# Gate products with the recurrent branch's four channel groups and both layers' modulation products placed between them

## What is computed

```
u = conv_b + sum(xp[:, j:j + s] * conv_w[j] for j in range(C_CONV))
r = sigmoid(einsum(u, wa) + ba);  i = sigmoid(einsum(u, wx) + bx)
log_a = -LRU_C * r * softplus(-lam)
a = exp(log_a)
gated_in = sqrt(-expm1(2.0 * log_a)) * (i * u)
hs = associative_scan(combine, (a, gated_in))
y_c = hs * gelu(yc)
gates = sigmoid(gt + b_gate)                       # gt: 3072 of the columns of h @ w_in
mod = silu(cond) @ w_ada + b_ada                   # once for the even, once for the odd layer
shift, scale, gate = split(mod, 3)
```

## Time and profile before

| what | value |
|---|---|
| median of 3 runs | 4327.39 us (4327.06 to 4327.49) |
| the profiled execution's own time | 4331.49 us |
| its span in the trace | 4329.7 us |
| mean granted TensorE clock | 0.915 of full speed |
| PE busy, share of the span | 3607.7 us, 83% |
| DVE busy | 2302.6 us, 53% |
| ACT busy | 1458.5 us, 34% |
| POOL busy | 296.1 us, 7% |
| DMA | 229.97 MB, mean 53 GB/s |

### The profile page before, as it was taken

One profiled execution on the slowest core, in us unless ns is written; L12 is line 12 of the kernel. 1 busy time (PEld: TensorE's weight loads), 2 busy tenths in 40 slices (PEclk: granted clock), 3 DMA queues, 4 the chain that ended last, 5 costly groups with the idle time before them and its releaser, 6 DMA issues. The chain is left out here.

```text
span 4329.7 us, 44928 instructions
## 1 busy us (share of the span) xinstructions
PE 3607.7 (83%) x18492; PEld 2935.6 (68%) x18492; DVE 2302.6 (53%) x3898; ACT 1458.5 (34%) x2559; POOL 296.1 (7%) x379
## 2 busy tenths in 40 slices
PE   3799996877797999999789877877697888868877
PEld 2588885655675888888567666766575777756666
DVE  4899444666644222223555646656544666435554
ACT  3221133544212111111443534444323444423431
POOL 2121200000101000000100000000001000000000
PEclk9899968988898999999899989999797999988999
DMA  2133331000520111111201000000220010100111
GB/s 83 31 120 121 113 125 56 26 20 10 195 102 27 52 49 40 46 44 46 83 27 32 22 31 26 25 31 21 96 73 33 29 34 29 35 18 18 31 60 62
DMA packets 69292, 229.97 MB, mean 53 GB/s; under 512 B 8472, under 2 KB 12568, under 8 KB 69088
## 3 DMA queue, kind: packets, MB, share of 16 engines
q1 hardware_dynamic: 43056, 132.68, 9.3%
q0 software_dynamic: 22576, 81.85, 5.5%
q10 hardware_dynamic: 3456, 12.58, 0.8%
HBM read 180.42 MB, written 36.17 MB: 50 GB/s over the span
## 5 line engine op out<-in xcount | busy, mean ns | idle before, releaser
L2139 PE MATMUL PS<-m,m 128*128 128x512 f32 (+2 forms) x3560 | 1418.8, 399 | 286.9 <-DVE m L2483 54.9
L2140 PE MATMUL PS<-m,m 128*128 128x512 f32 (+2 forms) x3560 | 1378.1, 388 | 0.0
L2141 PE MATMUL PS<-m,m 128*128 128x512 f32 (+2 forms) x3560 | 1377.5, 387 | 0.0
L2139 PEld LDWEIGHTS PS<-m,m 128*128 128x128 f32 (+1 forms) x3560 | 687.5, 193 | 482.4 <-issue 111.5
L2141 PEld LDWEIGHTS PS<-m,m 128*128 128x128 f32 (+1 forms) x3560 | 687.5, 193 | 135.6
L2140 PEld LDWEIGHTS PS<-m,m 128*128 128x128 f32 (+1 forms) x3560 | 690.1, 194 | 119.6 <-issue 2.7
L2483 DVE TENSOR_TENSOR m<-m,m 128x1024 fp32r<-128x1024 f32 (+4 forms) x203 | 207.8, 1024 | 417.0 <-ACT m L2316 416.2
L2768 DVE TENSOR_TENSOR m<-PS,m 128x512 fp32r<-128x512 f32 x352 | 241.1, 689 | 287.4 <-ACT m L2410 286.9
L2410 ACT CAST m<-PS 128x512 fp32r<-128x512 f32 x352 | 205.6, 588 | 513.7 <-PE PS L2238 512.1
L2229 PE MATMUL PS<-m,m 64*128 64x256 f32 (+5 forms) x1968 | 257.8, 373 | 85.0 <-ACT m L2399 57.9
L2229 PEld LDWEIGHTS PS<-m,m 64*128 64x128 f32 (+1 forms) x1968 | 218.0, 201 | 130.8 <-ACT m L2399 73.7
(11 more groups left out here) (203 smaller groups left out, 3980.8 us busy)
## 6 DMA issues: line engine op xcount, KB each, us to landing
m<-in_w SPq DMA_DIRECT2D x220, 512.0 KB, 3.3
g_scratch<-m ACTq DMA_DIRECT2D x24, 512.0 KB, 2.8
m<-g_scratch POOLq DMA_DIRECT2D x24, 512.0 KB, 4.7
m<-in_w SPq DMA_DIRECT2D x32, 256.0 KB, 2.7
x_scratch<-m POOLq DMA_DIRECT2D x2, 4096.0 KB, 12.3
m<-m POOLq DMA_DIRECT2D x60, 128.0 KB, 2.7
y_scratch<-m POOLq DMA_DIRECT2D x12, 512.0 KB, 2.9
m<-y_scratch POOLq DMA_DIRECT2D x12, 512.0 KB, 5.3
```

The lines of the kernel that those rows point to most:

```text
L2139: pe.e.engine.matmul(o, L[0], X[0], start=start, stop=False)
L2140: pe.e.engine.matmul(o, L[0], X[1], start=False, stop=False)
L2141: return pe.e.engine.matmul(o, L[1], X[0], start=False, stop=stop)
```

## The change

The modulation products of both layers, 48 in all, stand inside the 24 gate products, two in each: one after the fourth of the eight steps of each half. Their weights go through a ring of two tiles of its own. The odd layer's tiles no longer go through `raw`. The four channel groups of the recurrent branch stand at the gate products 15, 17, 19 and 21 (counted from 0): `conv` is issued before the gate product, `lrugate`, `scan` and `y_store` after it. `cond` and `decay` stand ahead of `topk`. `r` now lies in the tile `xc[c]`, and the result y in `gl[c]`. The `ready` steps are gone.

```diff
+LRU_AT = [15, 17, 19, 21]
-MOVES, GATE_STORES, RING = 12, 4, 6
+MOVES, GATE_STORES, RING = 12, 4, 2
-    order = [x for x in weight_tiles() if x[0][:2] != "ea"]
+    order = [x for x in weight_tiles() if x[0][:2] not in ("ea", "oa")]
...
             m8 = [mem([P, 8]) for _ in range(2)]
+            c8, nc8, sa, sb_, sc_, sd_ = (mem([P, 4]) for _ in range(6))
+            p.add("cond", csil=csil[:, :], cond=vc("cond", 0, 16))
+            p.add("decay", lam=vc("lam", 0, 4), ...)
             for b0 in (2, 4, 6):
                 p.add("topk", b0=b0, score=score, m8=m8)
...
-            u, r, i_, a_, th, yc = ring = [mem([P, T]) for _ in range(6)]
-            p.add("cond", csil=csil[:, :], cond=vc("cond", 0, 16))
+            u, i_, a_, th = (mem([P, T]) for _ in range(4))
+            ring = [mem([P, T]) for _ in range(RING)]
+            m_all = [(kind, m_) for kind in ("ev", "od") for m_ in range(24)]
+            def m_fetch(n):
+                kind, m_ = m_all[n]
+                p.add("eload", n=n, out=ring[n % RING][:, :], ...
+                      signal=S.ring[n % RING], free=[(S.mod, m_all[n - RING])] if n >= RING else [])
             def modulate(n):
-                for m_ in m_order[:n]:
-                    get, kt, release, event = w_get(f"oa{m_}")
...
+                p.add("mod", of=kind, m=m_, L=[ring[n % RING][:, 128 * k:128 * k + 128] for k in range(8)],
+                      o=PS[:, at_:at_ + 2], csil=csil, after=(S.ring[n % RING], ("ea", n)))
+                if n + RING < 48:
+                    m_fetch(n + RING)
+            def lru_conv(c):
                 p.add("conv", c=c, ...)
-                modulate(6)
+            def lru_scan(c):
+                r = xc[c][:, 3:3 + T]
...
-                p.add("scan", c=c, ..., yc=yc[:, :], ..., free=t_y)
-                t_y = [y_store(4 + c, yc, T, [(S.lru, ("y", c))])]
+                p.add("scan", c=c, ..., yc=gl[c][:, :], ..., free=[])
+                y_store(4 + c, gl[c], T, [(S.lru, ("y", c))])
+            for n in range(RING):
+                m_fetch(n)
+            for n_g in range(24):
...
+                if n_g in LRU_AT:
+                    lru_conv(LRU_AT.index(n_g))
+                for n, _ in enumerate(linear_steps(f"gt{i}_{d}", h_rhs, CH1, ev_s)):
+                    if n % 8 == 3:
+                        modulate(2 * n_g + n // 8)
+                g_free[x] = [move(g_d[8 * i + d], gd[:, :], g_t, on="act")]
+                if n_g in LRU_AT:
+                    lru_scan(LRU_AT.index(n_g))
-            p.add("ready", on="act", after=[(S.lru, "decay"), ring_done])
-            p.add("ready", on="dve", after=[ring_done])
```

More of the change, by code:

```diff
@@ L1166, in schedule @@
             m8 = [mem([P, 8]) for _ in range(2)]
+            c8, nc8, sa, sb_, sc_, sd_ = (mem([P, 4]) for _ in range(6))
+            p.add("cond", csil=csil[:, :], cond=vc("cond", 0, 16))
+            p.add("decay", lam=vc("lam", 0, 4), c8=c8[:, :], nc8=nc8[:, :], sa=sa[:, :], sb=sb_[:, :], sc=sc_[:, :],
+                  sd=sd_[:, :])
             for b0 in (2, 4, 6):
@@ L1184, in schedule @@
                 gl_t.append(e1.events)
-            u, r, i_, a_, th, yc = ring = [mem([P, T]) for _ in range(6)]
-            p.add("cond", csil=csil[:, :], cond=vc("cond", 0, 16))
+            u, i_, a_, th = (mem([P, T]) for _ in range(4))
+            ring = [mem([P, T]) for _ in range(RING)]
             m_bank = {"ev": 6, "od": 7}
-            m_order = list(range(24))
-            def modulate(n):
-                for m_ in m_order[:n]:
-                    get, kt, release, event = w_get(f"oa{m_}")
[L1193 to L1233, removed]
-            p.add("ready", on="act", after=[(S.lru, "decay"), ring_done])
-            p.add("ready", on="dve", after=[ring_done])
-            t_y = []
-            for c in range(4):
+            m_all = [(kind, m_) for kind in ("ev", "od") for m_ in range(24)]
@@ new lines, in m_fetch @@
+            def m_fetch(n):
+                kind, m_ = m_all[n]
+                at_ = W_AT[f"{kind[0]}a{m_}"][0]
+                p.add("eload", n=n, out=ring[n % RING][:, :], in_=w[at_:at_ + P * 1024].rearrange("(p c) -> p c", p=P),
+                      signal=S.ring[n % RING], free=[(S.mod, m_all[n - RING])] if n >= RING else [])
+            def modulate(n):
+                kind, m_ = m_all[n]
+                at_ = 512 * m_bank[kind] + 2 * m_
+                p.add("mod", of=kind, m=m_, L=[ring[n % RING][:, 128 * k:128 * k + 128] for k in range(8)],
+                      o=PS[:, at_:at_ + 2], csil=csil, after=(S.ring[n % RING], ("ea", n)))
+                if n + RING < 48:
+                    m_fetch(n + RING)
@@ L1247, in schedule, with ev_s @@
                         bank_free[b] = [(S.evac, n)]
-                p.add("scan", c=c, gates=(S.evac, n), a=a_[:, :], r=r[:, :], th=th[:, :], i=i_[:, :], u=u[:, :], yc=yc[:, :],
-                      gl=gl[c][:, :], c8=c8[:, c:c + 1], nc8=nc8[:, c:c + 1], free=t_y)
-                t_y = [y_store(4 + c, yc, T, [(S.lru, ("y", c))])]
+                p.add("scan", c=c, gates=(S.evac, n), a=a_[:, :], r=r, th=th[:, :], i=i_[:, :], u=u[:, :], yc=gl[c][:, :],
+                      gl=gl[c][:, :], c8=c8[:, c:c + 1], nc8=nc8[:, c:c + 1], free=[])
+                y_store(4 + c, gl[c], T, [(S.lru, ("y", c))])
+            for n in range(RING):
+                m_fetch(n)
+            g_free = [[], []]
+            for n_g in range(24):
+                d, i, x = n_g // 3, n_g % 3, n_g % 2
+                gd, gf, g_t = gate[x], g_free[x], []
+                def ev_s(o, t0, tn, done):
+                    n = p.id()
+                    p.add("sigmoid", n=n, d=gd[:, t0:t0 + tn], o=o, bias=vc("b_gate", 8 * i + d),
+                          after=[done] + gf)
+                    g_t.append((S.evac, n))
+                    return [(S.evac, n)]
+                if n_g in LRU_AT:
[6 more added lines that the diff above has]
+                    lru_scan(LRU_AT.index(n_g))
             st["lo"] = "dve"
```

## The result

The changed kernel takes **4295.5 us** (median of 4 runs, 4291.23 to 4297.89) against 4327.4 before: ratio 0.9925, 95% interval 0.991 to 0.9941. It is 31.9 us faster; 24.2 were forecast, and the time lies inside the stated range. The profiled execution took 4297.19 us, 34.3 less than that of before. Of these, 34.6 us are gained ahead of attention A, whose first product starts at 640.88 instead of 675.48 us. From there to the end of the span it was 3654.2 us before and is 3654.5 us.

What follows compares the result with a forecast made beforehand. PE's gate products set the pace to 557 us, then 118.4 us ran at clock 0.62 with idle engines. 603.3 + 10.6 + 2.5 + 13.7 + 10.8 + 6.5 + 3.9 gave 651.3, 24.2 us earlier: 4303.2 us, range 4284 to 4316.

Steps and rivals of the forecast that it cites:

- The gate products with two modulations: Gate products on PE: each takes 10.88 + 2 x 1.84 = 14.56 us, and 24 take 349.4 us.
- The loads are covered: Loads for ring tiles during gate products: landing in 4.5 us, issued 14.56 us ahead, costed at nothing; cover 10 us.
- The rival of the ring of two: Each of the 24 gate products waits 1.0 us for loads, 24 us in all: 4327 us, no change; chance 0.05.
- The first convolution: Behind gate product 15: DVE's convolution ends at 497.3, PE waits 10.6 us, and 2.5 us more go to the clock.
- The waits for POOL: Before products 17, 19, 21, 23: PE waits for POOL's subtraction behind the y store, 3.0 us three times, 1.8 once: 10.8 us.
- I take 3.48 for the first three groups: POOL's subtraction after the y store takes 3.48 us beside DVE's convolution, 2.40 alone for the last group.
- The rival in which POOL is held: The convolution's three DVE operations hold POOL's subtraction; PE waits 5.6 us at three places: 4312 us, chance 0.10.
- the one in which the store does not hold the weights: PE runs through from group 0 on, so 10.8 + 6.5 us are not lost: 4286 us, chance 0.13.
- The clock behind these waits: PE's clock is lost after the pauses for POOL: 2 us after each of three, half a microsecond after the short one, 6.5 us.
- The end: Fence before attention A waits for the last gate tile's store, 3.9 us, so attention A starts at 651.3.
- Sum: PE ends at 647.4 us; attention A starts at 651.3 instead of 675.48, 24.2 us earlier.
- The rival of the lower clock: The clock stays low from product 16 on, 14.2 us for each of eight products: 4410 us, chance 0.05.

Runs made afterwards that it cites:

- the base run: The changed kernel measured again without any edit, beside the follow-up variants: 4294.02 us, ratio 0.9928 to the kernel before.
- the reordered store: Against the changed kernel, the store of y is issued behind the next subtraction on POOL: 4288.85 us, ratio 0.9917 to the kernel before.

## Why the prediction was right, point by point

- *The gate products with two modulations.* 14.57 us, forecast 14.56. They started 0.7 us later than before, by variation of the stage ahead of them: PE's restart at 164.36 came at 165.01 here, and at 164.36 in the base run.
- *The loads are covered.* No wait for a load in the profile. The rival of the ring of two is excluded for this order. A ring of more tiles was not tried on the chip.
- *The first convolution.* End 497.6, forecast 497.3; the pause was 9.7 us for 10.6, mostly since product 15 ended some 0.9 us later. (The forecast's own dates, 486.9 and 497.3, give 10.4.) That `decay` took 7.1 us for 7.0 is luck: up to ACT's exp it was 1.9 us for 3.1, and from there 5.2 for 3.9, since a DVE operation of 128x4 waited 2.2 us beside POOL's subtraction. That the date of this convolution makes the pause is shown by moving the groups to 16. The eight matmuls behind it took 4.98 us where those of group 1 took 3.03, so 1.9 us were lost to the clock instead of 2.5.
- *The waits for POOL.* Right in place, number and cause, which the reordered store shows. The size was wrong: 5.9 us for 10.8. The step that failed is "I take 3.48 for the first three groups": the subtraction took 2.37, and DVE was held instead. With 2.40 for all four the forecast's own working gives 1.8 us each, 7.2 us, which is what they cost from start to start. The rival in which POOL is held falls by the same rows, and the one in which the store does not hold the weights by the four waits.
- *The clock behind these waits.* The term of 6.5 us was the largest error. It was taken for pauses of 3 us, so it hung in part on the same 3.48 us; at 1.8 us the forecast would still have given 3.5 to the clock. Pauses of 1.5 us did not cost it: the matmuls behind the first of them start 0.23 us apart (519.66, 519.89). Where the pauses were 3.3 us, with the odd modulations behind, three of four cost it: over the six microseconds from the restart the granted clock was 0.51, 0.72, 0.72 and 1.00.
- *The end.* The fence's pause was 3.56 us for 3.9, by the store of the last gate, as forecast.
- *Sum.* Attention A was forecast at 651.3 and came at 640.88, 10.4 us earlier. Of this 6.5 are the clock, 4.9 POOL, 0.9 the pause, 0.6 its restart and 0.3 the fence, against 0.7 of later start and some 2 us more. 1.3 of these are the waits for POOL again: from the second matmul of product 16 to that of product 17 it is 519.66 - 503.29 = 16.37 us, 1.80 more than the 14.57 without a wait, while the idle time is 1.48. The rest, under 1 us, is not placed. So the places and causes were right; the two sizes behind POOL's queue, the length of the subtraction and the clock that a short pause costs, make nearly all of the 10.4 us, close to a third of the gain.
- *The median* gained 31.9 us where the profile gained 34.3. The part behind attention A varies between profiles of one and the same kernel by 2.7 us, and the granted clock differs in it; which pause there decides was not tried.
- *The rival of the lower clock* did not happen, but it is real: two modulations in a row are enough to lower it in some products. That they stood apart, one in each half, is a part of the gain.

DVE and POOL where the first subtraction behind a store meets the convolution:

```profile
516.79 3.57 DVE L2614 SCALAR_TENSOR_TENSOR m<-m,m,m 128x1024 f32<-128x1024 f32 x1
...
521.71 1.29 DVE L2614 SCALAR_TENSOR_TENSOR m<-m,m,m 128x1024 f32<-128x1024 f32 x1
```

```profile
522.38 2.87 POOL L2875 TENSOR_TENSOR m<-m,m 128x1024 fp32r<-128x1024 f32 x1 [3.11 <-ACT m L2314]
```

The Trainium skill, page "SBUF — State Buffer", section "Who interferes with whom", says that in such a pair one side is blocked wholly by who came first. That one side is blocked wholly agrees with the rows: the first of the three convolution operations alone took 3.57 us where the last took 1.29, 2.28 more beside a subtraction of 2.37, and the scan took 4.34 - 2.29 = 2.05 more. That it is the one who came later agrees in part. The scan at 513.51 came behind the subtraction at 513.23 and was held. The next subtraction here, at 522.38, came 0.67 us behind the convolution's last operation; that one kept its 1.29 us, and the subtraction took 2.87. But at 516.79 the DVE operation stands 0.10 us ahead of the subtraction at 516.89, and it was DVE that was held. The range was drawn as if POOL were the side that loses; where PE's wait hung on it, it wasn't.

## What to carry to other kernels

Work that stands where its engine would wait anyway costs little, and moving it alone gains nothing: the odd modulations were hidden behind a chain of DVE and ACT. The chain in its turn needed something on PE to hide behind. Either move alone was slower than no move (1.005 and 1.010), both together 0.9925. After such a move, read the waits by line and ask of each pause for its date and its queue: one index and one issue moved behind another gave a further 19 us.

## What was not expected of the hardware

- Where GpSimd's subtraction started 0.1 us behind a VectorE operation with inputs from SBUF, GpSimd's kept its length (2.37 us) and VectorE's took 3.57 us for 1.29, so that the three of the convolution took 6.21 for 3.93, in all three places of the changed kernel. Where the subtraction came 0.67 us behind such an operation, it took 2.87 us and VectorE's kept its length.
- One modulation product of 1.84 us between dense products left the granted clock at 1.00 over 220 us; two in a row lowered it to 1.2 GHz in some of the products, and the mean to 0.93.
